# Mixture-of-experts blocks: how gathered rows are fetched and in which tiles the expert matrices come

## What is computed

```python
logits = t @ w_router                          # t: 256 x 1024, normalised tokens
top_logit, top_idx = top_k(logits, 2); gate = softmax(top_logit)
# tokens sorted by expert, padded, one expert per block of rows x_blk
y_blk = (silu(x_blk @ w1[e]) * (x_blk @ w3[e])) @ w2[e]   # w1, w3: 1024 x 2816, w2: 2816 x 1024
y[token] += y_blk * gate
```

## Time and profile before

| | |
|---|---|
| median of 3 runs | 1534.47 us (1533.12 to 1538.61) |
| profiled execution, its own time | 1538.68 us |
| its span, first to last instruction | 1536.8 us |
| mean granted TensorE clock | 0.968 |
| busy share of the span | PE 93%, PEld (weight loads) 76%, DVE 74%, ACT 58%, POOL 22% |
| DMA | 374.65 MB, mean 244 GB/s |
| chain that ended last | PE 73%, DVE 11%, ACT 6%, issue 6% |

### The profile page before, as it was taken

One profiled execution on the slowest core, in us unless ns is written; L12 is line 12 of the kernel. 1 busy time (PEld: TensorE's weight loads), 2 busy tenths in 40 slices (PEclk: granted clock), 3 DMA queues, 4 the chain that ended last, 5 costly groups with the idle time before them and its releaser, 6 DMA issues.

```text
span 1536.8 us, 24138 instructions
## 1 busy us (share of the span) xinstructions
PE 1435.5 (93%) x8701; PEld 1173.8 (76%) x8701; DVE 1141.0 (74%) x1098; ACT 896.8 (58%) x988; POOL 333.7 (22%) x427
## 2 busy tenths in 40 slices
PE   4788889999998999898999999999999999999995
PEld 3567768788887777677787888888878888888884
DVE  6964657655545556476898889888898899888985
ACT  4334454544435354544776767776677677676774
POOL 3995650999200067200000000000000000000000
PEclk9898889999999999998999999999999999999997
DMA  9242135565554423194999999999999999999970
GB/s 268 84 165 70 56 99 175 171 190 189 192 175 142 160 70 111 57 359 157 337 365 330 364 331 348 362 331 352 364 316 364 334 349 361 319 364 326 350 265 27
DMA packets 273810, 374.65 MB, mean 244 GB/s; under 512 B 17617, under 2 KB 220753, under 8 KB 273617
## 3 DMA queue, kind: packets, MB, share of 16 engines
q1 hardware_dynamic: 270176, 367.51, 71.1%
q0 software_dynamic: 1280, 3.15, 1.1%
q10 hardware_dynamic: 2288, 3.11, 0.7%
HBM read 371.63 MB, written 1.05 MB: 242 GB/s over the span
## 4 chain that ended last, share of the span: by engine, by line
PE 73%; DVE 11%; ACT 6%; issue 6%; DMA 1%; SPq 1%; POOL 1%; ACTq 0%; DVEq 0%; POOLq 0%
PE bank L578 71%; ACT hi L1047 4%; DVE lo L1407 3%; SPq L453 1%; PE bank L977 1%; PE bank L596 1%; DVE raw L1486 1%; DVE raw L393 1%; DVE at_lo L1824 1%; DVE raw L395 1%; DMA raw<-in_w_out_dram 1%; DMA areg<-in_norm_mix_dram 1%; DVE at_lo L1794 1%; DVE bank L1479 0%; POOL raw L1943 0%
## 5 line engine op out<-in xcount | busy, mean ns | idle before, releaser
L1407 DVE TENSOR_TENSOR lo<-raw,hi 128x2048 fp32r<-128x2048 f32 x347 | 804.2, 2322 | 213.9 <-ACT hi L1047 205.1
L1047 ACT ACTIVATE hi<-raw 128x2048 fp32r<-128x2048 f32 x347 | 663.0, 1914 | 134.0 <-PE bank L578 131.4
L578 PE MATMUL bank<-hi,at_hi 128*128 128x512 f32 x1280 | 522.4, 408 | 36.0 <-DVE lo L1407 10.7
L578 PE MATMUL bank<-lo,at_hi 128*128 128x512 f32 x1280 | 507.4, 396 | 0.0
L578 PE MATMUL bank<-hi,at_lo 128*128 128x512 f32 x1280 | 507.3, 396 | 0.0
L578 PEld LDWEIGHTS bank<-hi,at_hi 128*128 128x128 f32 x1280 | 245.6, 192 | 92.3 <-DVE lo L1407 16.7
L578 PEld LDWEIGHTS bank<-hi,at_lo 128*128 128x128 f32 x1280 | 245.1, 191 | 53.3
L578 PEld LDWEIGHTS bank<-lo,at_hi 128*128 128x128 f32 x1280 | 245.9, 192 | 47.0
L578 PE MATMUL bank<-hi,ht_hi 128*128 128x512 f32 x440 | 172.7, 392 | 4.4 <-DVE ht_lo L1725 3.5
L578 PE MATMUL bank<-hi,ht_lo 128*128 128x512 f32 x440 | 171.8, 390 | 0.0
L578 PE MATMUL bank<-lo,ht_hi 128*128 128x512 f32 x440 | 171.7, 390 | 0.0
(11 more groups left out here) (248 smaller groups left out, 1112.7 us busy)
## 6 DMA issues: line engine op xcount, KB each, us to landing
raw<-in_moe_w_dram SPq DMA_DIRECT2D x528, 512.0 KB, 5.4
raw<-in_ffn_w_dram SPq DMA_DIRECT2D x66, 512.0 KB, 4.3
raw<-in_w_in_dram SPq DMA_DIRECT2D x64, 512.0 KB, 4.5
raw<-in_w_branch_dram SPq DMA_DIRECT2D x16, 512.0 KB, 4.1
raw<-in_w_out_dram SPq DMA_DIRECT2D x16, 512.0 KB, 6.4
raw<-in_w_glu_dram SPq DMA_DIRECT2D x4, 512.0 KB, 4.2
xres<-in_x_dram SPq DMA_DIRECT2D x2, 512.0 KB, 6.1
areg<-in_norm_mix_dram ACTq DMA_DIRECT2D x2, 512.0 KB, 6.7
```

Source lines behind the costliest of these rows:

```text
L578: return pe.matmul(o, a, b, start=start, stop=stop)
L1047: act.activation(hi[:, slot, :], src, ACT.Copy).then_inc(hi_ready, 1)
L1407: tt(lo[:, slot, :], src, hi[:, slot, :].bitcast(f32), SUB).then_inc(lo_ready, 1)
```

## The change

Four things change together, all in the expert part.

- **Rows of further blocks.** The first block's rows are still gathered by products. Before the experts start, GpSimd writes the normalised tokens to a DRAM tensor of 257 rows, `xn_rows`, whose last row is zero. For each following block TensorE multiplies `place` by a column of constants (256 minus the token's number), VectorE turns that into the row number per slot (`slot_row`, 256 for an empty slot), GpSimd fetches the 128 rows with one indirect DMA (512 KB) over xn's SBUF space, and TensorE turns them with eight transposes into PV. The row numbers are made in step 3 of a block, the rows turned in step 4 (a turn of the loop has steps 1 to 6, and 6 is step 0 of the next block).
- **Up matrices in tiles of 512 columns.** A block has NEC = 6 chunks: five of 512 columns with tiles w1a, w1b, w3a, w3b, w2a, w2b, and one of 256 with ka, kb (w1 and w3 side by side, as before) and w2. It is 33 tiles as before, in another order (`expert_order`), with the up tiles of chunk c+1 running in step c.
- **Separate banks.** w1's products go to PJ[0], w3's to PJ[1] (the narrow chunk has both in PJ[0]). Silu and product work on 512 columns, and four transposes follow, or two in the narrow chunk. w1a waits until the silu of the chunk before is read out (`g_ready`); w1a of the next block waits for the narrow chunk's product (`h_done`) and for the fetched rows.
- **Order on ScalarE and VectorE.** VectorE's step begins with the product of its chunk. The transposed gate matrix gets a buffer of its own, and `place` is turned after step 1 instead of 3.

The diff's core (TensorE, ScalarE, VectorE and GpSimd; "..." marks what is left out):

```diff
+EC, NEC = 512, 6
+def expert_order():
+    steps = []
+    for c in range(NEC):
+        if c + 1 == NEC:
+            steps.append([("w1a", c + 1), ("w1b", c + 1), ("w3a", c + 1), ("w2", c), ("w3b", c + 1)])
+        elif c + 2 == NEC:
+            steps.append([("ka", c + 1), ("kb", c + 1), ("w2a", c), ("w2b", c)])
+        else:
+            steps.append([("w1a", c + 1), ("w1b", c + 1), ("w3a", c + 1), ("w2a", c), ("w2b", c), ("w3b", c + 1)])
+    return steps
+STEPS = expert_order()
+FIRST_TILES = [("w1a", 0), ("w1b", 0), ("w3a", 0), ("w3b", 0)]
+STEP_AT = [len(FIRST_TILES) + sum(len(STEPS[i % NEC]) for i in range(c)) for c in range(NEC + 2)]
 PJ_PER_LAYER = 15
...
+        xg = xn[:, 0, :]
...
+                s = moe_slot(j)
+                if kind[0] == "k":
+                    k0 = 0 if kind == "ka" else KD // 2
+                    dst = raw[:, s, :].rearrange("p (k w c) -> p k w c", w=2, c=FC)
+                    load(s, [(dst[:, :, i, :], w[k0 * P:(k0 + 4) * P, c * EC:c * EC + FC].rearrange("(k p) c -> p k c", p=P))
+                             for i, w in enumerate((m1, m3))])
+                elif kind[:2] == "w2":
+                    load(s, split_k(s, m2, c * EC // P + (2 if kind == "w2b" else 0), 0, D))
+                else:
+                    load(s, split_k(s, m1 if kind[:2] == "w1" else m3, 0 if kind[2] == "a" else KD // 2, c * EC, EC))
...
+            def slot_rows(b):
+                pe.wait_ge(place_ready, b + 2)
+                pe.wait_ge(gt_ready, b + 1)
+                for th in range(TH):
+                    m = mm(TR[1][:, 0:1], place[:, th, :], cst[:, C_ROW + th:C_ROW + th + 1], th == 0, th == 1)
+                m.then_inc(slot_full, 1)
+            def rows_t(b):
+                pe.wait_ge(xg_in, b * 16 + 16)
+                for k in range(KD):
+                    m = pe.transpose(banks[4 + k // 4][:, (k % 4) * P:(k % 4 + 1) * P], xg[:, k * P:(k + 1) * P], ident)
+                    if k % 4 == 3:
+                        m.then_inc(xe_full, 1)
+            def up(b, at, bank, half):
+                s = (T_MOE + at) % SPLITS
+                pe.wait_ge(lo_ready, b * FFN_TILES + (T_MOE + at + 1))
                 for k in range(4):
...
-                for f in range(2):
-                    m = pe.transpose(TR[0][:, f * P:(f + 1) * P], v_flat[:, FC + f * P:FC + (f + 1) * P], ident)
+                    pe.wait_ge(x_added, b * 4 + 9)
+                for f in range(h_width(c) // P):
+                    m = pe.transpose(TR[0][:, f * P:(f + 1) * P], v_flat[:, f * P:(f + 1) * P], ident)
...
-                        m = three(banks[2 + n][:, :], ht_hi[:, f, 0:P], ht_lo[:, f, 0:P],
+                        m = three(banks[2 + n][:, :], ht_rows_hi[:, f0 + f, :], ht_rows_lo[:, f0 + f, :],
...
-                    mm(bank[:, :], ht_hi[:, th, P:2 * P], at_hi[:, 4 * n:4 * n + 4, P:2 * P], True, False)
-                    mm(bank[:, :], ht_hi[:, th, P:2 * P], at_lo[:, 4 * n:4 * n + 4, P:2 * P], False, True).then_inc(comb_full, 1)
...
+                    mm(bank[:, :], gate_t[:, th, :], at_hi[:, 4 * n:4 * n + 4, P:2 * P], True, False)
+                    mm(bank[:, :], gate_t[:, th, :], at_lo[:, 4 * n:4 * n + 4, P:2 * P], False, True).then_inc(comb_full, 1)
+            def place_t(b):
+                pe.wait_ge(x_added, b * 4 + 12)
+                for th in range(TH):
+                    pe.transpose(TR[1][:, th * P:(th + 1) * P], place[:, th, :], ident)
+                for th in range(TH):
+                    m = mm(TR[1][:, TH * P:TH * P + 1], place[:, th, :], column[:, 1, th:th + 1], th == 0, th == 1)
+                m.then_inc(pg_full, 1)
...
-                if c == NCH:
-                    combine(b)
+                for n, (kind, chunk) in enumerate(STEPS[c % NEC]):
+                    at = STEP_AT[c] + n
+                    if kind[:2] == "w2":
+                        at = FFN_TILES - 1 if final and kind == "w2" else at
+                        down(b, c, at, kind)
+                        if c == NEC and kind == "w2a":
+                            combine(b)
+                    elif not (final and chunk == NEC):
+                        if kind in ("w1a", "ka"):
+                            if c == NEC - 1:
+                                pe.wait_ge(h_done, b * NEC + (2 * NCH + c + 1))
+                                pe.wait_ge(xe_lo_ready, 2 * b + 3)
+                            else:
+                                pe.wait_ge(g_ready, b * NEC + (2 * NCH + c + 1))
+                        if kind == "w1b" and c == NEC - 1:
+                            pe.wait_ge(xe_lo_ready, 2 * b + 4)
+                        up(b, at, PJ[1] if kind[:2] == "w3" else PJ[0], 0 if kind[-1] == "a" else 1)
+                    if n == 0:
+                        hidden_t(b, c)
+                        if c == 3 and not final:
+                            slot_rows(b)
+                        if c == 4 and not final:
+                            rows_t(b)
+                if c == 1:
+                    place_t(b)
...
-                up(0, 0, half)
+                up(0, half, PJ[0], half)
+            for half in range(2):
+                up(0, 2 + half, PJ[1], half)
...
                                    ACT.Copy).then_inc(xe_hi_ready, 1)
             def silu(b, c):
...
-                act.wait_ge(tile_used, b * FFN_TILES + (T_MOE + (3 * c if c > 0 else 1) + 1))
-                act.activation(v_flat[:, 0:FC], h_bank(c)[:, 0:FC], ACT.Silu).then_inc(g_ready, 1)
...
+            def hidden_hi_of(b, c):
+                act.wait_ge(ht_tr, b * NEC + (NCH + c + 1))
+                act.activation(ht_rows_hi[:, 0:h_width(c) // P, :], TR[0][:, 0:h_width(c)].rearrange("p (f s) -> p f s", s=P),
+                               ACT.Copy).then_inc(ht_hi_ready, 1)
...
             def expert_step(b, c, final=False):
-                if c == NCH:
-                    result_hi(b, b * FFN_TILES + (T_MOE + FFN_TILES + 2))
-                if c == 4:
+                at, following = STEP_AT[c], STEP_AT[c + 1]
+                if not (final and c == NEC - 1):
+                    split_to(b, at + 2, final)
+                if c == 2:
...
-                if c >= 0:
-                    split_moe(b, FFN_TILES - 1 if final and c == NCH - 1 else 3 * c + 4)
-                    hidden_hi(b * NCH + (NCH + c + 1), P)
-                if not (final and c + 2 >= NCH):
-                    split_moe(b, 3 * c + 5)
-                if not (final and c + 1 >= NCH):
-                    silu(b, c + 1)
-                if c == NCH - 2 and not final:
+                hidden_hi_of(b, c)
+                if final and c == NEC - 1:
+                    return
+                split_to(b, at + 3, final)
+                silu(b, c + 1)
+                if c == NEC - 2 and not final:
                     gathered(b + 2)
-                if not (final and c + 2 >= NCH):
-                    split_moe(b, 3 * c + 6)
+                for i in range(at + 4, following + 2):
+                    if c == NEC - 1 and i == following + 1:
+                        result_hi(b, b * FFN_TILES + (T_MOE + place_in_step(c, "w2") + 1))
+                    split_to(b, i, final)
...
-            expert_step(0, -1)
+            split_moe(0, 2)
+            split_moe(0, 3)
+            split_moe(0, 4)
+            silu(0, 0)
+            split_moe(0, 5)
...
             def hidden(b, c):
-                dve.wait_ge(g_ready, b * NCH + (2 * NCH + c + 1))
-                dve.wait_ge(ht_tr, b * NCH + (NCH + c))
-                tt(v_flat[:, FC:2 * FC], v_flat[:, 0:FC], h_bank(c)[:, FC:2 * FC], MUL).then_inc(h_done, 1)
+                dve.wait_ge(g_ready, b * NEC + (2 * NCH + c + 1))
+                if h_width(c) == EC:
+                    dve.wait_ge(tile_used, b * FFN_TILES + (T_MOE + up_last(c) + 1))
+                right = PJ[1][:, 0:EC] if h_width(c) == EC else PJ[0][:, FC:2 * FC]
+                tt(v_flat[:, 0:h_width(c)], v_flat[:, 0:h_width(c)], right, MUL).then_inc(h_done, 1)
...
             def expert_step(b, c, final=False):
-                if c == NCH:
-                    result_lo(b)
-                if c >= 0:
-                    split_moe(b, FFN_TILES - 1 if final and c == NCH - 1 else 3 * c + 4)
-                    hidden_lo(b * NCH + (NCH + c + 1), P)
-                if not (final and c + 2 >= NCH):
-                    split_moe(b, 3 * c + 5)
-                if not (final and c + 1 >= NCH):
-                    hidden(b, c + 1)
-                if c == 5 and not final:
+                at, following = STEP_AT[c], STEP_AT[c + 1]
+                hidden(b, c)
+                if not (final and c == NEC - 1):
+                    split_to(b, at + 2, final)
+                hidden_lo_of(b, c)
+                if final and c == NEC - 1:
+                    return
+                split_to(b, at + 3, final)
...
+                if c == 2 and not final:
                     dve.wait_ge(gt_ready, b + 1)
```

(77 more changed lines are left out.)

66 lines of the change are left out of this document (40 added, 26 removed).

## The result

| | before | after |
|---|---|---|
| median of 11 runs each (range) | 1533.99 us (1531.92 to 1540.07) | 1540.54 us (1539.12 to 1542.36) |
| profiled execution, its span | 1538.68, 1536.8 | 1542.36, 1540.5 |
| mean granted clock of TensorE | 0.968 | 0.964 |

The ratio is 1.0039, with a 95% interval of 1.0028 to 1.005: 6.5 us slower. Against the bound of 0.5% that is no change; with eleven runs on each side the interval lies above 1 all the same.

The account below looks back on a forecast made before the run. TensorE was taken to set the pace, with the DMA following. Blocks +2.7, start and end -1.1, -1.1 and -1.2, and clock falls +6.4 summed to +5.7 us, from 1534.5 to 1540, range 1525 to 1558.

Parts of the forecast that it names:

- two new waits: TensorE waits once per block for VectorE's product, 2.83 us ahead of w1a and 0.77 us ahead of chunk 0's transposes.
- price of a fall: A stretch of 3.4 us with TensorE at half clock, taken to cost 1.6 us, at most 1.7.
- The wait ahead of w1a: TensorE waits 2.83 us before the next block's w1a, because hidden(5) stands behind two lo splits on VectorE.
- The second wait: After w2(5), TensorE waits 0.77 us for hidden(0) of 512 columns, ahead of its transposes.
- What goes and comes on TensorE: Per block, gather (3.57) and two old waits (1.08) go; row transposes (0.96) and slot product (0.48) come: 3.2 us gained.
- Start and end: First block's wait for lo goes, -1.1; last idle falls from 2.00 to about 1.0, -1.1; half clock behind it goes, -1.2.
- The clock: TensorE's clock falls to half behind four of the seven new waits ahead of w1a, bounds 0 and 7: +6.4 us.
- The second case: No clock fall behind TensorE's new waits, because the idle time is split or too short: 1533.8 us; chance 0.18.
- The transfer: Indirect transfer of 512 KB per block taken at 7 us, bounds 5.4 and 13.6, hidden under 12.1 us of cover.
- The fourth case: Fetched rows arrive late ahead of TensorE's row transposes, each microsecond late costing seven: 1565 us at 15 us; chance 0.20.
- The third case: Faster: the two new waits don't form and the 3.2 us per block are kept: 1509 us; chance 0.14.
- The sum: Whole kernel: 2.7 - 1.1 - 1.1 - 1.2 + 6.4 = +5.7 us, 1540 us laid on the median; chance 0.48.

Follow-up runs that it names:

- Experiment 1: Changed kernel with VectorE making the narrow chunk's product ahead of the gathered rows and the two lo splits: 1513.31 us, ratio 0.9858 to before.
- experiment 5: Changed kernel with the narrow chunk's product ahead of gathered rows and splits, result_lo right behind hidden(0), result_hi one split later: 1509.37 us, ratio 0.9829 to before.
- Experiment 2: Changed kernel with eight matmuls of unused results ahead of TensorE's wait for the narrow chunk's product: 1533.56 us, ratio 0.9993 to before.
- experiment 8: Changed kernel with the eight transposes of the fetched rows moved into step 3, ahead of w3b: 1578.51 us (two runs), ratio 1.028 to before.
- experiment 4: Changed kernel with the old gather in place of slot products, indirect transfer and row transposes; new tiles, banks and order stay: 1559.3 us, ratio 1.0172 to before.
- experiment 3: Kernel before with only the fetched rows (slot products, indirect transfer, eight transposes), its tiles, banks and orders kept: 1520.25 us, ratio 0.9915 to before.

## Why the prediction was right, point by point

1540 was forecast and 1540.54 measured, on the side where it was given. The two new waits, their cause and the price of a fall came out as forecast. That the total agrees within 1 us is luck: several terms were off and made up for each other, and the profiles put the change at +7.7 us where the medians have +6.5.

- **The wait ahead of w1a**: forecast 2.83, measured 2.84, and by the named cause. Experiment 1 settles that: with the product ahead of the splits it is gone.
- **The second wait**: forecast 0.77, measured 0.65; experiment 5 takes it away and gains 0.55 per block.
- **What goes and comes on TensorE**: the four slot passes and the rows, from the trace of after (start, duration; the matmul behind each shows where they end):

```profile
987.04 0.50 PE L633 MATMUL bank<-cst,vreg 128*128 128x1 f32 x4
...
1004.28 1.04 PE L1023 MATMUL bank<-cst,qk 128*128 128x128 f32 x8
1005.07 0.48 PE L633 MATMUL bank<-hi,at_hi 128*128 128x512 f32 x1
```

The rows take 1005.07 - 1004.28 = 0.79 and a slow start, where 0.96 was taken. Altogether a block without a fall has 100.3 against 100.05: +0.26, forecast +0.39.
- **Start and end**: forecast -1.1, -1.1 and -1.2. In the first block the 1.67 us of the earlier trace rows is gone and 0.6 stands ahead of the first transposes, as named; at the end the 2.00 of the earlier trace rows has become

```profile
PE bank L633 <- DVE ht_lo L1923: 0.9, 1, 0.9
```

(forecast 1.0), and the clock stays at 1.00 behind it. From the expert part, 7.7 - 7 x 0.26 - 6 x 1.6 = -3.7 is left for both, forecast -3.4.
- **The clock, the mis-sized term**: 4 falls taken, 6 in the profile, so 9.6 us instead of 6.4; the price of one, 1.6, was right. This count is of the slowest of eleven executions; the others may have had fewer. Experiment 2 shows it as a cost of its own. The second case, no fall, was wrong in its count. On idle time the page "TensorE: Matmul & The Clock Gate" of the Trainium skill ("Why this matters for your kernels") warns from about 3 us on; here 1.92 us was followed by the lower clock five times of seven, so the measurement decides against the page.
- **The transfer, mis-sized but hidden**: 7 us taken. The issues of line 2105 (min/median/max ns on POOL, then from issue to landing):

```profile
L2105 POOL DMA_INDIRECT qk<-xn_rows,slot_row x7: 943/2952/3017, 789.2 to 1398.9; - x7
...
DMA to landing us min/median/max: 8.2/8.9/9.8
```

Around 1000 us the row number starts at 991.89 and takes 0.15, POOL starts at 993.03, the rows are there at 1001.91 and wanted at 1004.28. So 9.9 of about 12.2 us of cover are used: 2.4 us were spare in this block, where I had counted 5. In the seven blocks it was 1.4 (799.06 against 800.46) to 3.0. The fourth case (late, one for one) was nearer than its twice-the-largest-landing argument made it; experiment 8 confirms its mechanism.
- **The third case** (faster, no new waits, 1509) did not come about, but experiment 5 is that kernel with two edits of the order, at 1509.37. My bound of 22 + 3.4 us is 7 x 2.96 = 20.7 for the blocks there and 3.6 for start and end (expert part 777.9 us).
- **The sum** against the expert part was 5.7, measured 7.7: the clock gives +3.2 of the difference, the blocks -0.9, start and end -0.3.

## What to carry to other kernels

On an engine that works in order, the one short instruction that the bounding engine waits for goes ahead of long work that is wanted later: here 0.4 us of product behind two splits of 2.2 us cost 27 us in 1540. When a change is worth little, run its parts alone: one half gained 13.5 us and the other lost 25.5. And price a wait of TensorE of about 2 us or more at its length and, more often than not, a stretch at half clock behind it: in the loops here 26 of 35 waits of 1.9 to 2.9 us ahead of w1a had one, at 1.6 us each.

## What the runs showed of the hardware that was not expected

- **The length of an idle time does not alone decide whether the clock falls.** At the same place, once per block: 0.97 us, 0 falls of 7; 1.92, 5 of 7; 2.37, 5 of 7; 2.84, 6 of 7 (after), 7 of 7 (experiment 4) and only 3 of 7 in experiment 8, where a wait for the rows ends 15 to 17 us ahead of each (behind those, 6 of 6 at 3.6 to 4.4 us and none at 2.16). At the end, 2.00 us once with the earlier trace rows and once without (experiment 3); at the start, 1.67 us without. Ahead of the last combine all ten kernels idle 2.89 us, and the clock fell at its matmuls in five (before and experiments 1 to 4), not in the other five. The falls at these idle times began from 0.6 us ahead of TensorE's restart to 1.5 us behind it. What else decides stays open.
- **The indirect transfer** of 128 rows of 4 KB took 8.2 to 9.8 us to land at 342 to 366 GB/s in all, more than a direct one of the same 512 KB (5.3, the median); POOL began 0.8 to 1.1 us after the row number was written.
- **The issue of the indirect transfer ended only after VectorE's split.** It held POOL for 2.9 to 3.0 us in six blocks and 0.94 in the seventh. The first three rows are of after, the last two of experiment 3:

```profile
992.87 2.29 DVE L1505 TENSOR_TENSOR lo<-raw,hi 128x2048 fp32r<-128x2048 f32 x1 [0.83 <-ACT hi L1131]
993.03 2.95 POOL L2105 DMA_INDIRECT qk<-xn_rows,slot_row  x1 [98.97 <-DVE slot_row L1959]
...
1398.94 0.94 POOL L2105 DMA_INDIRECT qk<-xn_rows,slot_row  x1 [98.79 <-DVE slot_row L1959]
...
977.89 2.29 DVE L1430 TENSOR_TENSOR lo<-raw,hi 128x2048 fp32r<-128x2048 f32 x1
978.82 2.18 POOL L2017 DMA_INDIRECT qk<-xn_rows,slot_row  x1 [95.66 <-DVE slot_row L1870]
```

Where POOL began while a split was running (0.2 us into it in after, 0.8 to 1.0 in experiment 3), the issue ended 0.8 to 0.9 us after that split did; where both began within 0.01 us (the split at 1398.93) it took 0.94. The other kernels with this transfer show the same. The prediction had no row of POOL beside a split. The rows of that seventh block still landed 8.4 us after the start of the issue, so a shorter issue did not by itself bring them sooner.
